# Sample rows in four column quarters with a summing matmul, and the samples' key products on DVE

## The reference

```python
h = rmsnorm(x, ln1_g)
u, va, q, k, v = split(h @ w_in)               # 1024 x 2560, five groups of 512 columns
q, k = rope(q), rope(k)                        # 8 heads of 64
a = u * (causal(w_s) @ rmsnorm(va) + b_s)      # gating inside chunks of 128 positions
b = merge over dilations 1, 4, 16 of softmax(q k^T / 8) v   # samples: 3 x 128 cached keys and the own one
x = x + concat(a, b) @ w_out
x = x + moe(rmsnorm(x, ln2_g))                 # top 1 of 4 groups, top 2 of 8 gated experts in it
y = rmsnorm(x, lnf_g)
```

## Time and profile before

| | |
|---|---|
| median of 3 runs | 493.48 us (491.23 to 494.23) |
| profiled execution | 491.77 us, of it span 489.9 us |
| granted TensorE clock | 0.92 |
| PE busy | 393.8 us, 80% |
| DVE busy | 242.9 us, 50% |
| ACT busy | 156.7 us, 32% |
| POOL busy | 77.2 us, 16% |

### The profile page before, as it was taken

One profiled execution on the slowest core, in us unless ns is written; L12 is line 12 of the kernel. 1 busy time (PEld: TensorE's weight loads), 2 busy tenths in 40 slices (PEclk: granted clock), 3 DMA queues, 4 the chain that ended last, 5 costly groups with the idle time before them and its releaser, 6 DMA issues. The chain is left out here.

```text
span 489.9 us, 5994 instructions
## 1 busy us (share of the span) xinstructions
PE 393.8 (80%) x2254; PEld 204.4 (42%) x2254; DVE 242.9 (50%) x442; ACT 156.7 (32%) x315; POOL 77.2 (16%) x91
## 2 busy tenths in 40 slices
PE   0999996994898999987989999544999999978200
PEld 0554442441343444443544555443555555535000
DVE  1967457999568584545363222470222222211187
ACT  4723121233236475533432111301222222211142
POOL 0000203652220100000000000103233333311100
PEclk9999997999799999998999999755999999989855
DMA  8683413948401922610016791894599999993194
GB/s 300 220 275 106 148 49 101 365 137 279 151 1 43 344 67 82 219 65 1 1 43 258 260 383 44 308 409 156 205 383 411 412 409 407 406 401 137 57 346 171
DMA packets 39202, 104.88 MB, mean 214 GB/s; under 512 B 5656, under 2 KB 6552, under 8 KB 39168
## 3 DMA queue, kind: packets, MB, share of 16 engines
q1 hardware_dynamic: 32736, 90.00, 49.6%
q0 software_dynamic: 5856, 12.81, 7.0%
q10 hardware_dynamic: 576, 1.64, 1.0%
HBM read 97.87 MB, written 14.81 MB: 230 GB/s over the span
## 5 line engine op out<-in xcount | busy, mean ns | idle before, releaser
L1393 PE MATMUL bank<-weights_split,tokens_split 128*128 128x512 f16 (+1 forms) x744 | 175.1, 389 | 6.1 <-DVE big L1108 2.5
L1393 PEld LDWEIGHTS bank<-weights_split,tokens_split 128*128 128x128 f16 (+1 forms) x744 | 69.9, 97 | 97.5 <-issue 15.1
L1633 PE MATMUL bank<-big,tokens_split 128*64 128x256 f32 x384 | 47.4, 402 | 7.3 <-DMA big<-in_w_up 5.8
L591 POOL TENSOR_TENSOR big<-big,middle 128x1536 f32<-128x1536 f32 x8 | 27.7, 3466 | 103.7 <-DMA middle<-sample_q 53.9
L1633 PEld LDWEIGHTS bank<-big,tokens_split 128*64 128x64 f32 x384 | 30.5, 145 | 20.9 <-issue 8.8
L1299 DVE TENSOR_TENSOR middle<-bank,middle 128x128 f32<-128x128 f32 x16 | 4.7, 291 | 66.3 <-ACT middle L866 66.3
L1368 PE MATMUL bank<-ident,big 128*128 128x128 f32 (+1 forms) x92 | 14.7, 295 | 16.7 <-DVE big L945 12.0
L772 ACT ACTIVATE middle<-bank 128x128 f32<-128x128 f32 (+3 forms) x32 | 13.9, 433 | 38.7 <-PE bank L1441 38.7
L607 POOL DMA_DIRECT2D h_rows<-middle x5 | 2.7, 535 | 148.8 <-DVE middle L1188 148.8
L1441 PE MATMUL bank<-ident,middle 128*128 128x128 f32 x80 | 15.5, 291 | 11.5 <-DVE middle L1023 11.4
L935 DVE SCALAR_TENSOR_TENSOR weights_split<-middle,weights_split 128x1024 f16<-128x1024 f32 x16 | 19.1, 1220 | 10.4 <-ACT weights_split L687 10.4
(11 more groups left out here) (186 smaller groups left out, 551.2 us busy)
## 6 DMA issues: line engine op xcount, KB each, us to landing
big<-in_w_gate SPq DMA_DIRECT2D x12, 1024.0 KB
big<-in_w_up SPq DMA_DIRECT2D x12, 1024.0 KB
big<-in_w_down SPq DMA_DIRECT2D x12, 1024.0 KB, 11.7
middle<-in_w_in SPq DMA_DIRECT2D x16, 512.0 KB, 5.6
big<-in_cache_win_k SPq DMA_DIRECT2D x24, 256.0 KB, 3.9
middle<-in_cache_win_v SPq DMA_DIRECT2D x24, 256.0 KB, 4.2
big<-in_w_out SPq DMA_DIRECT2D x8, 512.0 KB, 6.9
big<-expert_rows SPq DMA_DIRECT2D x8, 512.0 KB, 7.2
```

What stands on the lines that cost most here:

```text
L591: nc.gpsimd.tensor_tensor(prod[:, :, :], kring[:, b % 2], qb[:, b % 2, :].unsqueeze(1).to_broadcast([P, NPAT, W]), ALU.mult).then_inc(prod ...
L1393: ins = T.matmul(out, (hT if rows is None else rows)[:, high_low, k if rows is None else k - 4, tokens], wg[:, place, part, k, columns], s ...
L1633: ins = T.matmul((ptb, ovb)[b][e * CAP:(e + 1) * CAP, 0:2 * FE], xT[:, b, k, e * CAP:(e + 1) * CAP], places[slot][:, 0:2, e, k * FE:(k + 1 ...
```

## The change

1. The sample tile's unit of each group is made in two steps. `sample_part`: the 8 high and 8 low rows of all samples stand beside each other in `samples_split` (32 columns, the rest zero) and are the stationary side; chunk 4h + j writes to the accumulator's partitions 32j to 32j + 31, so 16 matmuls of 512 columns in four column quarters. ACT copies the result to SBUF (`copy_part`). `sample_sum`: one f32 matmul with the constant `fold` adds the quarters and halves and gives the unit of 8 rows. This is done seven times: q, k, va, v, u and both halves of w_out.
2. POOL makes no products. `sum_prod` on DVE multiplies and then sums, samples 0 and 1 with k tiles 3 and 4, sample 2 behind va tile 3, samples 3 to 7 behind attention tasks 1, 3, 5, 7 and 9. The loads of keys 6 and 7 move behind the first two loads of values.
3. With fewer pieces in FILL (90 instead of 100) everything moves to other tasks. The samples' scores go from task 5 to 11, probabilities from 7 to 13, columns from 9 to 15; values of sample 0 from 8 to 12.
4. In the output projection the sample tile goes between tiles 2 and 3 (ROW_ORDER).

```diff
+UNITS = [("q", t) for t in range(NT - 1)] + [("part", "q"), ("k", 0), ("q", NT - 1)]
+UNITS += [("k", t) for t in range(1, NT - 1)] + [("part", "k"), ("va", 0), ("k", NT - 1)]
+UNITS += [("va", t) for t in range(1, NT - 1)] + [("part", "va"), ("v", 0), ("va", NT - 1)]
...
+FILL += [("part", "v", half) for half in range(2)]
+FILL += [("u", 0, part) for part in range(KD)] + [("sum", "v", 0)] + [("u", 1, part) for part in range(KD)]
+for _b, _rest in enumerate(([("u", 2.0)], [("u", 2.5), ("u", 3.0)], [("u", 3.5), ("part", "u"), ("mix", 0)],
+                            [("mix", 1), ("sum", "u"), ("mix", 2)], [("mix", 3)], [], [], [])):
     FILL += [("pv", _b, part) for part in range(NPAT)]
...
+VALUE_AFTER.setdefault(12, []).append(0)
+SUM_AFTER = {1 + 2 * i: 3 + i for i in range(NS - 3)}
...
-                nc.gpsimd.tensor_tensor(
-                    prod[:, :, :], kring[:, b % 2],
-                    qb[:, b % 2, :].unsqueeze(1).to_broadcast([P, NPAT, W]), ALU.mult).then_inc(prods, 1)
...
             def sum_prod(b):
 
+                dve.wait_ge(kq_in[b % 2], 64 * (b // 2 + 1))
+                V.tensor_tensor(prod[:, :, :], kring[:, b % 2],
+                                qb[:, b % 2, :].unsqueeze(1).to_broadcast([P, NPAT, W]), ALU.mult).then_inc(prods, 1)
                 dve.wait_ge(prods, b + 1)
...
-                if n == 9:
+                if n == 15:
                     sample_columns()
...
+            def sample_part(kind, place, half):
+
+                u = UNIT[("part", kind)]
+                if half == 0:
+                    free_wait(pe, u)
+                for part in range(2):
+                    for j in range(4):
+                        ins = T.matmul(acc[u % 2][32 * j:32 * j + 32, :], samples_split[:, 4 * half + j, :],
+                                       wg[:, place, part, 4 * half + j, :],
+                                       start=half + part == 0, stop=half + part == 2)
+                if half == 1:
+                    ins.then_inc(acc_ready, 1)
+
+            def sample_sum(unit, src):
+
+                u = UNIT[unit]
+                free_wait(pe, u)
+                T.matmul(acc[u % 2][0:NS, :], fold, src, start=True, stop=True).then_inc(acc_ready, 1)
...
+            project_out(2, 0)
+            left(pe, ("part", "out0"))
+            sample_sum(("out", 2 * NT - 2), part_out)
+            router(0)
+            h2_turns(1)
+            for half in range(2):
+                sample_part("out1", 0, half)
+            project_out(2, 1)
+            left(pe, ("part", "out1"))
+            sample_sum(("out", 2 * NT - 1), part_out)
+            router(1)
+            h2_turns(2)
+            project_out(3, 0)
```

279 lines of the change are left out of this document (171 added, 108 removed).

## The result

| | before | after |
|---|---|---|
| median | 492.88 us (491.23 to 494.23, 4 runs) | 504.47 us (503.41 to 505.76, 4 runs) |
| ratio | | 1.0269, 95% interval 1.0233 to 1.0304 |
| span of the profiled execution | 489.9 us | 502.1 us |
| granted TensorE clock | 0.920 | 0.893 |
| PE / DVE / POOL busy | 393.8 / 242.9 / 77.2 us | 384.7 / 239.4 / 49.8 us |

The kernel became 2.7% slower; 490 was forecast. The three engines of the last row do less than before, and the span is 12 us longer. Where the time goes is seen by stages. A stage runs from the first turning of one task to that of another, and the last one ends at the matmul of the ranks, which starts when DVE has done the routing. All starts are read from the timelines.

The account below looks back on a forecast made before the run. DVE was taken to set the pace before task 0, PE in the attention tasks, DMA in the experts. -8.4 + 8.2 - 6.0 + 5.5 - 1.5 = -2.2 from 491.77 us: 489.6, said as 490; range 478 to 500.

Parts of the forecast that it names:

- Bound and prices: Pace-setting engines, and prices: product 1.75 us, 16 quarter matmuls 1.4, f32 sum 0.5, a whole sample unit 1.9.
- A: Up to task 0: DVE no longer stands still for POOL and gets two pairs for four sums, -8.4 us.
- What bounds the kernel now: Opening reading of the old profile: DVE paces 82.0 to 123.3 us; PE's 3.47 and 5.41 us waits accompany POOL's products.
- B: Tasks 0 to 15: -0.6 in 0 to 10, then waits for columns, ACT and value split, and half clock; +8.2 us.
- rival 2: DVE's products within tasks delay PE; at 3.5 us each, 502. Late keys 6 and 7 act alike; chance 0.1.
- C: Tasks 16 to 27: less PE work -3.2, a wait and low clock gone -3.8, new DVE wait +1.0; -6.0 us.
- D: Tasks 28 to 31: PE gaps before samples 5, 6 and 7, waiting for value splits; +5.5 us.
- E: Output projection: two cheaper sample units, -7.4, partly offset by waits, clock and a 128-row last tile; -1.5 us.
- Rival 1: The waits of B and D don't come: 475 us, or 482.5 with half of each; chance 0.35.
- Rival 3: Quarter matmuls don't overlap on PE: 3.7 us instead of 1.4 on four units, +9.2, so 499; chance 0.1.

Follow-up runs that it names:

- e8: The changed kernel with keys and q of sample 6 loaded ahead of the values of samples 0 and 1: 500.2 us, ratio 1.0183 to the kernel before.
- e2: The kernel before with each product on DVE just ahead of its sum, nothing else changed: 491.4 us, ratio 0.9991.
- h1: The kernel before with filler matmuls of no use in three waits (task 0, sample norm's turning, routing): 488.6 us, ratio 0.9946.
- g3: The changed kernel with filler matmuls of no use in its nine longest new waits: 493.9 us, ratio 1.0024 to the kernel before.
- the mended kernel: The changed kernel with earlier keys, sums, scores and columns, value pieces spread, and later turnings of gating tile 3 and tile 2: 487.5 us, ratio 0.9917.

## Why the prediction was wrong

**Bound and prices.** Right: product 1.753 us and sum 1.753 (said 1.75), DVE's 512-column operations at 0.69 again. `sample_part` takes 1.05 us for 16 matmuls, not 1.4: the quarters do overlap. The Trainium skill (TensorEngine Tiling (Array Packing), Theoretical Speedup) gives up to four times; against the earlier trace rows's 0.232 us each it is 3.5 here. No row shows a price of changing the mode: the quarters start 1.00 us after a turning of 1.07 us, and the next unit starts 0.98 us after them (287.51, 288.51, 289.49). The f32 sum was underestimated, 1.03 us instead of 0.5, so a unit costs 2.1, not 1.9. The error is in the reading of the earlier trace rows: the profile lists every f32 matmul of this program twice. `sample_sum` has one matmul and its row says x2; `mix` has two of 256 columns and its row says x4, so the 16 of the earlier trace rows are 8, at 0.51 us each, and 512 columns take 1.03. The rows of the timeline of after (L1587 is `mix`, L1469 the sum, L1459 the quarters):

```profile
213.62 1.03 PE L1587 MATMUL bank<-big,middle 128*128 128x256 f32 x4
...
284.74 1.03 PE L1469 MATMUL bank<-middle,small 128*8 128x512 f32 x2
...
288.51 1.05 PE L1459 MATMUL bank<-weights_split,samples_split 128*32 128x512 f16 x16
```

**A, -8.4:** -8.7. The chain was read rightly, from the waits of the k tiles to DVE's list: va begins at 76.83 us, said 77, and the rope of the sample keys at 84.89, said 85. One reading in "What bounds the kernel now" was too strong. PE's waits of 3.47 and 5.41 us were mostly not POOL's: without a product on POOL, PE still waits 3.97 us for the rope of k tile 3 and 4.52 ahead of task 0.

**B, +8.2:** +10.4. Tasks 11 to 15 came as worked out (the wait is 4.88 us, said 4.9; the stage +8.3, said +8.8). The step that failed is tasks 0 to 10 (+2.1, said -0.6): the keys of sample 6 came 2.70 us late. The forecast named late keys in rival 2, which had a tenth as a whole; in e8, with the keys early, the stage is 2.8 us shorter, which is all of the miss as far as one execution of each can tell. The data was in the diff: keys 6 and 7 moved behind two sets of values.

**C, -6.0:** -3.2. PE's busy time fell by 3.5 us (44.1 to 40.6), and the wait of 2.50 went as said. Two things came in its place. Four waits for DVE's scaling, 0.60, 1.20, 1.41 and 1.56 us in the timeline of after, make 4.8 us where the kernel before has 2.1 beside the 2.50: +2.7 for the +1.0 of the forecast. And the stage begins at 1.2 GHz behind the wait for the columns: its first turning and scores take 0.90 and 1.65 us, which at 2.4 GHz take 0.55 and 0.92. The comparison also leans on one execution: in e2 and h1, whose code is the same in this stage, it takes 47.2 us and not 48.7, since behind the wait of 2.50 the clock held.

**D and E, +4.0:** +13.2. This is the term that sank the forecast. Up to the first unit of the output projection (at 243.90 before, 253.09 after) D came to +10.7 for +5.5, and E to +2.5 for -1.5. (By its own terms, -4.9, +3.3, +1.0 and the gaps of 5.7, D should have read +5.1.) The gaps in D came about as long as said: 1.56 and 1.01 us ahead of sample 5 for 2.4, 0.86 for 1.1 ahead of sample 6, 2.40 for 2.2 ahead of sample 7. Not counted were 1.56 us ahead of a turning of a gating tile (252.62). In E 1.79 us stand ahead of the turning of tile 2, said 2.9, and 4.03 ahead of the last norm, where the kernel before waited 1.70; the +1.3 for the last tile's 128 rows took a part of that. What was missed above all is the clock: I charged 1.5 us in B and 1.0 in E, and nothing behind the gaps of D. The four rows of E at the low clock alone (299.49, 301.25, 320.99, 323.64) are 5.6 us longer than at 2.4 GHz, and g3 gives 7.7 us back in D and E together. A reason to count it was there: the row behind the 2.50 us wait in the earlier trace rows takes 1.43 us for three matmuls, and I used it as a gain only. It was no certain sign, as e2 shows (0.81 us behind the same wait).

**Rivals.** Rival 1 (waits don't come) is out: they came. Rival 2's dear product is out (e2), its late keys came. Rival 3 is out (1.05 us). The chances were set on whether the waits come, and not on what each draws after it; no rival went above 502, and the range, 478 to 500, left even that out.

**Still open.** Tasks 11 to 15 of the mended kernel (18.7 us for 16.4) were not followed further. Why the clock holds behind one wait and falls behind another of the same length is not shown either. How much of the tail's clock hangs on the waits and how much on the small f32 matmuls around them was not parted: the fillers show only that work in the waits brings it back.
